# The decode's K pages multiplied with their queries on GpSimd instead of VectorE

## The chip, the cores and the metric

The kernel runs on one core of one Trainium2 chip. The metric is the device time of one launch in microseconds (us), lower is better. The core's engines are named as the profile names them: PE is TensorE, ACT ScalarE, DVE VectorE, POOL GpSimd, and SP is the engine that only issues DMAs here.

## The reference

One inference step of a two-layer decoder, for 512 prompt positions and for 8 sequences that each decode one token. Layer 0 is a convolution module with memory attention and a dense SwiGLU; layer 1 is stick-breaking attention over shared K/V with memory attention, then top-2-of-8 experts. The change lies in layer 1's stick-breaking attention:

```python
z = jnp.einsum('bthd,bshd->bhts', q, k) * HEAD_DIM ** -0.5 + bias
log_keep = jnp.where(causal, jax.nn.log_sigmoid(-z), 0.0)
between = lax.cumsum(log_keep, axis=3, reverse=True) - log_keep
w = jnp.where(causal, jnp.exp(jax.nn.log_sigmoid(z) + between), 0.0)
o = jnp.einsum('bhts,bshd->bthd', w, v)
# prompt: q, k of 512 new positions, 12 heads of 64.
# decode: 8 sequences; k and v are cache_k[page_table], cache_v[page_table]: 2 pages of 128 positions each
```

For a decoding sequence z is one query row against 256 cached keys: per page and head, 64 products and their sum.

## The kernel before

It is a hand-scheduled program: each engine has one list of instructions written out in order, and semaphores alone tie the lists together. The stages follow one another over the whole core: the projections up to layer 1's queries (to about 844 us of the span), stick-breaking attention (844 to 944), memory attention of layer 1 (to about 1000), the output projection, routing and the experts.

**The prompt's attention** is cut into 36 units (`UNITS`), one head and one group of query/key blocks each; `QGROUPS` gives three groups of 4, 3 and 3 blocks of 128, so a unit has 512 or 384 columns. Units go in pairs (a visit `v` holds units 2v and 2v+1), and six units make a period. For each unit u the engines pass data around:

- PE `stick_scores` (L2730): z into a PSUM bank; then ACT `soft_exp` (L1260) writes exp(z) to `zc`, DVE `soft_clamp` (L2015) clamps it in place, ACT `soft_log` (L1266) takes ln(1 + .), DVE `soft_max` (L2023) reads PSUM and `zc` and writes `sp`, ACT `soft_high` (L1272) rounds it to `sph`, DVE `soft_low` (L2032) subtracts the two into `spl`.
- PE `stick_sums` (L2747, L2749) adds the running sums of `sph` and of `spl` to z, ACT `stick` (L1280) takes the weights `wt`, and PE `stick_values` (L2764) multiplies them with V.

PE's order in visit v is: scores of visit v+2, sums of units 2v and 2v+1, values of visit v-1. The scores of visit v+3 wait (`sb_w`) until ACT has made `wt` of unit 2v+1, since six PSUM banks go round (`ZBANKS`). ACT's order in step s is exp of unit s, ln of s-1, rounding of s-2, `wt` of s-3. DVE's is clamp of s, max of s-1, low part of s-2, then a piece of the decode's work. Every sixth step has one more small piece for PE's finished output on ACT and on DVE (L1717).

**The decode's scores** ride in DVE's list. `pgs` holds for each sequence n two pages of K, 128 x 768 values each, and a buffer `qb` of two holds the query, copied to all partitions. From step 7 (`PAGES_FROM`) on three steps belong to one sequence: first `page_product` (L2008) multiplies both pages in place, one instruction of 1536 columns, then `page_scores` (L1999) sums one page over each head's 64 columns, and in the third step the other. The SP list loads the K pages, the first two queries, and then for each n, once both sums of n are done (`qk`), the two V pages over the K pages of n and the query of n+2. After step 31 the 8 sequences' scores get their bias, exp, ln and sums in the last steps of the prompt's units. GpSimd's list holds between the two clearings of `wpad` (L857, L858) and a clearing after the last unit (L860) nothing.

Of the kernel before, what the change touches and what calls it, by code (L numbers as in the profile page):

```python
# [25 lines left out]
ACT = mybir.ActivationFunctionType  # L26
ALU = mybir.AluOpType
# [3 lines left out]
P = 128  # L31
# [3 lines left out]
B = 8  # L35
# [7 lines left out]
FS = NH * HD // P  # L43
# [5 lines left out]
NPG = 2  # L49
# [54 lines left out]
def build(nc, a, o):  # L104
# [3 lines left out]
    with ExitStack() as ctx:  # L108
        def at(name, shape, dt, offset):
            return nc.alloc_sbuf_tensor_at(name, shape, dt, offset=base0 + offset)  # L110

        def small(name, shape, dt=F32):
            return ctx.enter_context(nc.sbuf_tensor(name, shape, dt))

        def sem(name):
            return ctx.enter_context(nc.semaphore(name))
# [63 lines left out]
        pgs = at("pgs", [P, B, NPG, FS * P], F32, 49920)  # L180
        qrow = at("qrow", [P, D], F32, 29120)
        qb = [at("qb0", [P, FS * P], F32, A + 87680), at("qb1", [P, FS * P], F32, A + 52608)]
# [5 lines left out]
        class Mem:  # L188
# [57 lines left out]
        rstd = small("rstd", [P, T])  # L246
# [93 lines left out]

        u_zero, ud_new, cv, cd, cd_sum = map(sem, "u_zero ud_new cv cd cd_sum".split())
        cw_in, cw_row, u_sh, wb_dve, wb_pool, cg, ce, ce_dve, ln_acc = map(sem, "cw_in cw_row u_sh wb_dve wb_pool cg ce ce_dve ln_acc".split())
        ln_sum, ln_mean, ln_xc, ln_sq, ln_used, ln_root, ln_rstd, ln_y = map(
            sem, "ln_sum ln_mean ln_xc ln_sq ln_used ln_root ln_rstd ln_y".split())
        outs = sem("outs")

        mk_in, mc_in, mv_in = map(sem, "mk_in mc_in mv_in".split())
# [7 lines left out]
        pg_in = [sem(f"pg_in{n}") for n in range(B)]  # L355
        qb_in = [sem("qb_in0"), sem("qb_in1")]
        sel_ready, qd_out, qm_in, qk, wp_zero, sd_pv, mix_hi, mix_lo = map(
            sem, "sel_ready qd_out qm_in qk wp_zero sd_pv mix_hi mix_lo".split())
# [93 lines left out]
        def row_broadcast(src, shape_ap):  # L452
            return bass.AP(tensor=src.tensor, offset=src.offset, ap=[[0, P]] + shape_ap)
# [36 lines left out]
        PG_AT = [0, 1, 4, 7, 2, 3, 5, 6]  # L490
# [16 lines left out]
        def _(e):  # L507
# [111 lines left out]
            def load_pages(src, n):  # L619
                for g in range(NPG):  # L620
                    page = e.value_load(ptab[0:1, bass.ds(n * NPG + g, 1)], min_val=0, max_val=src.shape[0] - 1)
                    e.dma_start(pgs[:, PG_AT[n], g:g + 1, :], src[bass.ds(page, 1)].rearrange("n s c -> s n c"))\
                        .then_inc(pg_in[n], 16)

            def load_query(n):
                e.dma_start(qb[n % 2][:, :], row_broadcast(qdr[n, 0:FS * P], [[1, FS * P]])).then_inc(qb_in[n % 2], 16)
# [15 lines left out]
            e.wait_ge(v_out, 32)  # L642
            load_query(1)
            for n in range(B):
                e.wait_ge(qk, 3 * n + 3)
                load_pages(vp, n)
                if n + 2 < B:
                    load_query(n + 2)

            e.wait_ge(sb_z, UNITS)  # L650
            e.wait_ge(sb_c, UNITS)
# [92 lines left out]
        def _(e):  # L744
# [111 lines left out]
            e.wait_ge(qd_out, 32)  # L856
            e.memset(wpad[0][:, :], 0.0).then_inc(wp_zero, 1)  # L857
            e.memset(wpad[1][:, :], 0.0).then_inc(wp_zero, 1)  # L858
            e.wait_ge(sb_c, UNITS)
            e.memset(memB.pdp[:, :, :], 0.0).then_inc(wp_zero, 1)  # L860
            for g in range(U_OUTB - 1, U_END - 1):
# [23 lines left out]
            for i in range(NT + 1):  # L885
                n = P if i < NT else B
# [64 lines left out]
        def _(e):  # L951
# [67 lines left out]
            n = 0  # L1019
# [131 lines left out]
            e.activation(halves(rstd[:, :]), ps[:, 0:2, 0:HALF], ACT.Ln, scale=1.0 / (FS * P), bias=eps[:, :])\  # L1151
             .then_inc(ln_root, 1)
            e.wait_ge(ln_root, 1)
            e.activation(rstd[:, :], rstd[:, :], ACT.Exp, scale=-0.5).then_inc(ln_rstd, 1)
            e.wait_ge(mb_step, MB_S)
            for c in range(FM):
                ins = e.activation(planes(hh[:, FS + c, :])[:, :, TP // PH:TQ],
# [213 lines left out]
            for i in range(NT + 1):  # L1371
                n = P if i < NT else B
# [113 lines left out]
            for k in range(4):  # L1486
                c, n = k // 2, k % 2
                e.activation(eyh[:, c, 512 * n:512 * n + 512], ps[:, 2 + k, :], ACT.Copy, scale=gsl[:, c:c + 1]).then_inc(f_act, 1)
            early_hi(4)
            for i in range(NF):  # L1490
                n = P if i < NT else B
# [10 lines left out]
        def _(e):  # L1502
# [211 lines left out]
            def mix_low(k, src, hi):  # L1714

                e.wait_ge(mix_hi, hi)
                e.tensor_tensor(hl[:, k, 0:TP], src, hh[:, k, 0:TP].bitcast(F32), ALU.subtract).then_inc(mix_lo, 1)  # L1717
# [68 lines left out]
            def decode_low_planes(q, hi):  # L1786

                e.wait_ge(mix_hi, hi)
                for c in range(FM):
                    ins = e.tensor_tensor(planes(hl[:, FS + c, :])[:, :, TP // PH:TQ],  # L1790
                                          ps[:, q, 64 + c * B:64 + c * B + B].rearrange("p (t g) -> p g t", g=PH),
                                          planes(hh[:, FS + c, :].bitcast(F32))[:, :, TP // PH:TQ], ALU.subtract)
                ins.then_inc(mix_lo, 1)
# [90 lines left out]
            mix_low_planes(FS + 1, ps[:, 7, :], 2)  # L1884
            e.wait_ge(ln_root, 1)
            decode_low_planes(3, 3)
            e.wait_ge(ln_rstd, 1)
            for k in range(FS):
                e.tensor_tensor(conv_out(k), conv_out(k), planes(rstd[:, :]), ALU.mult).then_inc(ln_y, 1)

# [103 lines left out]
            def pages(ap):  # L1994
                return ap.rearrange("p (g r) -> p g r", g=NPG)

            def page_scores(n, g):

                e.tensor_reduce(zd[:, 0, 96 * g + NH * n:96 * g + NH * n + NH],  # L1999
                                pgs[:, PG_AT[n], g, :].rearrange("p (h d) -> p h d", d=HD), AX, ALU.add)\  # L2000
                 .then_inc(qk, 1)

            def page_product(n):

                e.wait_ge(pg_in[n], 32)
                e.wait_ge(qb_in[n % 2], 16 * (n // 2 + 1))
                page = pgs[:, PG_AT[n], :, :]
                e.tensor_tensor(page, page, qb[n % 2][:, :].unsqueeze(1).to_broadcast([P, NPG, FS * P]), ALU.mult)\  # L2008
                 .then_inc(qk, 1)

            def soft_clamp(u):

                z = zc[:, u % ZBANKS, 0:unit_cols(u)]
                e.wait_ge(sb_e, u + 1)
                e.tensor_scalar(z, z, EXP_MAX, None, ALU.min).then_inc(sb_zc, 1)  # L2015

            def soft_max(u):

                h, n = unit(u)[0], unit_cols(u)
                e.wait_ge(sb_l, u + 1)  # L2020
                if u >= SP_SLOTS:
                    e.wait_ge(sb_lo, u - SP_SLOTS + 1)
                e.scalar_tensor_tensor(out=sp[:, u % SP_SLOTS, 0:n], in0=unit_z(u), scalar=bias[:, 0, h:h + 1],  # L2023
                                       in1=zc[:, u % ZBANKS, 0:n], op0=ALU.add, op1=ALU.max).then_inc(sb_s, 1)

            def soft_low(u):

                n = unit_cols(u)
                e.wait_ge(sb_hi, u + 1)
                if u >= SPL_SLOTS:  # L2030
                    e.wait_ge(sb_c, u - SPL_SLOTS + 1)
                e.tensor_tensor(spl[:, u % SPL_SLOTS, 0:n], sp[:, u % SP_SLOTS, 0:n], sph[:, u % ZBANKS, 0:n].bitcast(F32),  # L2032
                                ALU.subtract).then_inc(sb_lo, 1)

            PAGES_FROM = 2 * NQ + 1
            for s in range(UNITS + 2):
                if s < UNITS:
                    soft_clamp(s)
                if 1 <= s <= UNITS:
                    soft_max(s - 1)  # L2040
                if s >= 2:
                    soft_low(s - 2)
                n, part = (s - PAGES_FROM) // 3, (s - PAGES_FROM) % 3
                if 0 <= n < B:
                    if part == 0:
                        page_product(n)
                    else:
                        e.wait_ge(qk, 3 * n + 1)
                        page_scores(n, part - 1)
                if s == PAGES_FROM + 3 * B:  # L2050
                    e.wait_ge(qk, 3 * B)
                    e.tensor_tensor(pages(zd[:, 0, :]), pages(zd[:, 0, :]), bias2, ALU.add).then_inc(sd_step, 1)
                if s == UNITS - 3:
                    e.wait_ge(sd_step, SD_E)
                    e.tensor_scalar(zd[:, 1, :], zd[:, 1, :], EXP_MAX, None, ALU.min).then_inc(sd_step, 1)
                if s == UNITS - 1:
                    e.wait_ge(sd_step, SD_L)
                    e.tensor_tensor(zd[:, 1, :], zd[:, 0, :], zd[:, 1, :], ALU.max).then_inc(sd_step, 1)
                if s % (2 * NQ) == 4 and s >= 10:
                    f = (s - 10) // (2 * NQ)  # L2060
                    mix_low(f, ps[:, 6 + f % 2, :], MIX_ALL + f + 1)
# [125 lines left out]
            for i in range(NT + 1):  # L2187
                n = P if i < NT else B
# [161 lines left out]
            for k in range(4):  # L2350
                c, n = k // 2, k % 2
# [7 lines left out]
            for i in range(NF):  # L2359
                n = P if i < NT else B  # L2360
# [708 lines left out]
```

## Time and profile before

| | |
|---|---|
| median of 3 runs | 1744.93 us (1742.52 to 1746.0) |
| the profiled execution, its own time | 1747.19 us |
| its span in the trace | 1745.4 us |
| busy over the span: PE, DVE, ACT, POOL | 93%, 55%, 43%, 31% |
| mean granted clock of TensorE | 0.962 |

The shares are averages over stages with different limits; PE is near full in the projections and experts, which are most of the span. For a change in one stage the rows of that stage count. Times in the rows are us from the span's start, a row of the timeline gives start, duration, engine, line, operation, output and inputs, shape, and in brackets how long the engine was idle before it and what ended that. A duration in the timeline overlaps the next one's start a little, so what an instruction takes of its engine's time is read from start to start.

### The profile page before, as it was taken

How to read it: one execution, taken by the hardware profiler on the slowest of the kernel's cores; microseconds unless marked ns; L12 is line 12 of the kernel's file. 1: busy time of each engine (PE TensorE's matmuls, PEld its weight loads, DVE VectorE, ACT ScalarE, POOL GpSimd, SP SyncE). 2: the span in 40 equal slices, each digit the busy share in tenths (PEclk: the TensorE clock that was granted, in tenths of full speed). 3: DMA queues.
4: the chain of work that ended last, by engine and by line, in shares of the span. 5: the costliest groups of instructions: out<-in, count | busy, mean ns of one | idle time of the engine just before them, and what ended most of it. 6: DMA issues, size and time to landing. Idle time of an engine off the chain costs nothing.

```text
span 1745.4 us, 29562 instructions
## 1 busy us (share of the span) xinstructions
PE 1617.6 (93%) x11452; PEld 1493.9 (86%) x11452; DVE 955.1 (55%) x1248; ACT 757.0 (43%) x1067; POOL 539.2 (31%) x333
## 2 busy tenths in 40 slices
PE   6898878999999999899888797999999999999998
PEld 5898758999999999898765495989898898989896
DVE  6796554311111001522595627868677686868686
ACT  6445453322222122431585325455454455545454
POOL 1001213345554444232000131624152423415172
PEclk9899889999999999999999798999999999999989
DMA  6634202254454552121555216987979697997961
GB/s 205 114 96 149 77 1 73 73 150 138 138 150 135 165 166 94 50 96 58 207 161 143 99 40 179 308 229 241 257 224 270 208 294 201 265 233 232 256 237 51
DMA packets 346271, 282.01 MB, mean 162 GB/s; under 512 B 9505, under 2 KB 311117, under 8 KB 346055
## 3 DMA queue, kind: packets, MB, share of 16 engines
q1 hardware_dynamic: 324947, 251.09, 49.5%
q10 hardware_dynamic: 18084, 18.14, 3.1%
q0 software_dynamic: 3168, 11.80, 2.2%
q8 instruction: 46, 0.75, 0.2%
q14 instruction: 26, 0.21, 0.0%
HBM read 246.62 MB, written 35.10 MB: 161 GB/s over the span
## 4 chain that ended last, share of the span: by engine, by line
PE 78%; DVE 11%; issue 4%; ACT 3%; POOL 2%; SPq 1%; DMA 1%; ACTq 0%; DVEq 0%; POOLq 0%
PE ps L2412 35%; PE ps L2974 15%; PE ps L2977 7%; PE ps L2398 3%; PE ps L2400 3%; PE ps L2399 3%; PE ps L3001 2%; PE ps L3000 2%; DVE cT L1671 2%; PE ps L2551 2%; DVE wlo L1547 1%; PE ps L2380 1%; PE ps L2561 1%; DVE spl L2032 1%; DVE sp L2023 1%
## 5 line engine op out<-in xcount | busy, mean ns | idle before, releaser
L2974 PE MATMUL ps<-ejx,ewh 128*128 128x384 f32 x1408 | 404.5, 361 | 3.6 <-DVE ejx L2223 1.9
L2209 DVE TENSOR_TENSOR ewl<-eraw,ewh 128x2048 fp32r<-128x2048 f32 (+1 forms) x144 | 304.1, 2112 | 155.7 <-ACT ewh L1389 155.5
L1389 ACT ACTIVATE ewh<-eraw 128x2048 fp32r<-128x2048 f32 (+1 forms) x144 | 255.2, 1773 | 259.2 <-PE ps L2977 151.9
L2977 PE MATMUL ps<-ejx,ewl 128*128 128x192 f32 x1408 | 353.8, 251 | 0.0
L2412 PE MATMUL ps<-hh,whi 128*128 128x260 f32 x1504 | 312.4, 289 | 21.1 <-DVE hl L1912 16.5
L2412 PE MATMUL ps<-hh,wlo 128*128 128x260 f32 x1504 | 307.8, 287 | 0.0
L2412 PE MATMUL ps<-hl,whi 128*128 128x260 f32 x1504 | 307.8, 287 | 0.0
L896 POOL TENSOR_TENSOR ea<-eat,ea 128x128 fp32r<-128x128 f32 x88 | 171.7, 1951 | 341.6 <-ACT ea L1447 341.3
L2974 PEld LDWEIGHTS ps<-ejx,ewh 128*128 128x128 f32 x1408 | 266.0, 189 | 7.0 <-issue 7.0
L2977 PEld LDWEIGHTS ps<-ejx,ewl 128*128 128x128 f32 x1408 | 270.6, 192 | 0.0
L2412 PEld LDWEIGHTS ps<-hh,whi 128*128 128x128 f32 x1504 | 238.1, 193 | 24.7 <-issue 15.9
L2412 PEld LDWEIGHTS ps<-hh,wlo 128*128 128x128 f32 x1504 | 237.1, 193 | 0.0
L2412 PEld LDWEIGHTS ps<-hl,whi 128*128 128x128 f32 x1504 | 237.0, 193 | 0.0
L785 POOL TENSOR_TENSOR wlo<-raw,whi 128x2048 fp32r<-128x2048 f32 x36 | 165.9, 4610 | 110.4 <-ACT whi L1226 72.5
L1945 DVE TENSOR_TENSOR tmp<-ps,rstd 128x520 f32<-128x520 f32 x44 | 30.7, 699 | 198.8 <-PE ps L2412 194.9
L779 POOL TENSOR_TENSOR wlo<-raw,whi 128x2048 fp32r<-128x2048 f32 x13 | 59.6, 4586 | 171.0 <-ACT whi L958 171.0
L2412 PE MATMUL ps<-acth,whi 128*128 128x260 f32 x352 | 72.0, 286 | 4.1 <-POOL actl L826 4.1
L826 POOL TENSOR_TENSOR actl<-tmp,acth 128x520 f32 (+1 forms) x22 | 29.2, 1328 | 137.7 <-ACT acth L1197 137.7
L2412 PE MATMUL ps<-actl,whi 128*128 128x260 f32 x352 | 71.6, 285 | 0.0
L2412 PE MATMUL ps<-acth,wlo 128*128 128x260 f32 x352 | 71.5, 285 | 0.0
L2398 PE MATMUL ps<-ewh,ea 128*128 128x512 f32 x176 | 70.5, 401 | 0.0
L3001 PE MATMUL ps<-ewl,ea 128*64 128x512 f32 x176 | 70.2, 399 | 0.0
(440 smaller groups left out, 2531.6 us busy)
## 6 DMA issues: line engine op xcount, KB each, us to landing
eraw<-in_w_gate_e SPq DMA_DIRECT2D x88, 512.0 KB, 4.8
eraw<-in_w_up_e SPq DMA_DIRECT2D x88, 512.0 KB, 6.0
eraw<-in_w_down_e SPq DMA_DIRECT2D x64, 512.0 KB, 6.0
eraw<-in_w_down_e SPq DMA_DIRECT2D x48, 256.0 KB, 2.9
xs<-zero ACTq DMA_DIRECT2D x10, 1152.0 KB, 4.8
raw<-in_w_gate_d SPq DMA_DIRECT2D x22, 512.0 KB, 4.1
raw<-in_w_up_d SPq DMA_DIRECT2D x22, 512.0 KB, 5.3
raw<-in_w_down_d SPq DMA_DIRECT2D x16, 512.0 KB, 4.6
```

Source lines behind the costliest of these rows:

```text
L779: e.tensor_tensor(out=wlo[:, s, :], in0=raw[:, s, :], in1=whi[:, s, :].bitcast(F32), op=ALU.subtract).then_inc(w_lo, 1)
L785: e.tensor_tensor(out=wlo[:, s, :], in0=raw[:, s, :], in1=whi[:, s, :].bitcast(F32), op=ALU.subtract).then_inc(w_lo, 1)
L896: e.tensor_tensor(out=ea[:, m, C + CB:2 * C], in0=eat[:, m % 2, 0:P], in1=ea[:, m, 0:P].bitcast(F32), op=ALU.subtract)
L1389: e.activation(ewh[:, s, 0:n], eraw[:, u % RAW, 0:n], ACT.Copy).then_inc(ew_hi, 1)
L2209: e.tensor_tensor(ewl[:, s, 0:n], eraw[:, u % RAW, 0:n], ewh[:, s, 0:n].bitcast(F32), ALU.subtract)\
L2398: e.matmul(dst, w_hi_, x_hi, start=first, stop=False, skip_group_check=check)
L2399: e.matmul(dst, w_hi_, x_lo, start=False, stop=False, skip_group_check=check)
L2400: return e.matmul(dst, w_lo_, x_hi, start=False, stop=last, skip_group_check=check)
L2412: ins = e.matmul(ps[:, 2 * q + h, 0:HALF], w, xx[:, k, h * HALF:(h + 1) * HALF], start=opens, stop=closes)
L2974: e.matmul(ps[:, q, 0:2 * C], ewh[:, s, o:o + P], ejx[:, k, :, :].rearrange("p h n -> p (h n)"), start=(k == 0), stop=(k == KD - 1), skip_ ...
L2977: ins = e.matmul(ps[:, q, C:2 * C], ewl[:, s, o:o + P], ejx[:, k, 0, :], start=False, stop=(k == KD - 1), skip_group_check=True)
L3001: ins = e.matmul(ps[0:CB, 2 + c, :], ea[:, k, P:C], wlm, start=False, stop=(k == KE - 1), skip_group_check=True)
```

## The change

GpSimd gets the products: right behind the two clearings of `wpad` it waits for the pages and the query of sequence n and multiplies page by page, two instructions of 768 columns each, each announced on a new semaphore `qp`. DVE keeps the sums, in the same two of the three steps; the third step of each sequence is left with no decode work. `qk` counts sums alone. On SP the query of n+2 is now loaded once both products of n are done, and stands ahead of the wait for the sums of n and the loads of its V pages. A semaphore of layer 0 (`ln_rstd`) is folded into another (`ln_root`), which pays for the new one.

```diff
@@ sync
             for n in range(B):
-                e.wait_ge(qk, 3 * n + 3)
+                if n + 2 < B:
+                    e.wait_ge(qp, 2 * n + 2)
+                    load_query(n + 2)
+                e.wait_ge(qk, 2 * n + 2)
                 load_pages(vp, n)
-                if n + 2 < B:
-                    load_query(n + 2)
@@ gpsimd
             e.memset(wpad[1][:, :], 0.0).then_inc(wp_zero, 1)
+            for n in range(B):
+                e.wait_ge(pg_in[n], 32)
+                e.wait_ge(qb_in[n % 2], 16 * (n // 2 + 1))
+                for g in range(NPG):
+                    page = pgs[:, PG_AT[n], g, :]
+                    e.tensor_tensor(page, page, qb[n % 2][:, :], ALU.mult).then_inc(qp, 1)
             e.wait_ge(sb_c, UNITS)
@@ scalar, layer 0
-            e.activation(rstd[:, :], rstd[:, :], ACT.Exp, scale=-0.5).then_inc(ln_rstd, 1)
+            e.activation(rstd[:, :], rstd[:, :], ACT.Exp, scale=-0.5).then_inc(ln_root, 1)
@@ vector, layer 0
-            e.wait_ge(ln_rstd, 1)
+            e.wait_ge(ln_root, 2)
@@ vector
-            def page_product(n):
-
-                e.wait_ge(pg_in[n], 32)
-                e.wait_ge(qb_in[n % 2], 16 * (n // 2 + 1))
-                page = pgs[:, PG_AT[n], :, :]
-                e.tensor_tensor(page, page, qb[n % 2][:, :].unsqueeze(1).to_broadcast([P, NPG, FS * P]), ALU.mult)\
-                 .then_inc(qk, 1)
...
-                if 0 <= n < B:
-                    if part == 0:
-                        page_product(n)
-                    else:
-                        e.wait_ge(qk, 3 * n + 1)
-                        page_scores(n, part - 1)
+                if 0 <= n < B and part:
+                    e.wait_ge(qp, 2 * n + part)
+                    page_scores(n, part - 1)
                 if s == PAGES_FROM + 3 * B:
-                    e.wait_ge(qk, 3 * B)
+                    e.wait_ge(qk, 2 * B)
```

On DVE, at the first sequence, the list of before reads as follows (`zc` is the clamp, `sp` the max, `spl` the low part; L2008 is the product of both pages, L1999 the sum of one):

```order
L2032 TENSOR_TENSOR spl<-sp,sph 128x384 [waits sb_c,sb_hi]
L2008 TENSOR_TENSOR pgs<-pgs,qb_101 128x1536 [waits qb_in0,pg_in0]
L2015 TENSOR_SCALAR zc<-zc 128x384 [waits sb_e]
L2023 SCALAR_TENSOR_TENSOR sp<-ps,bias,zc 128x512 [waits sb_lo,sb_l]
L2032 TENSOR_TENSOR spl<-sp,sph 128x512 [waits sb_c,sb_hi]
L1999 TENSOR_REDUCE zd<-pgs 128x12 [waits qk]
L2015 TENSOR_SCALAR zc<-zc 128x384 [waits sb_e]
```

And the list of the change at the same place (all lines are shifted, L2007 is the sum):

```order
L2032 TENSOR_TENSOR spl<-sp,sph 128x384 [waits sb_c,sb_hi]
L2015 TENSOR_SCALAR zc<-zc 128x384 [waits sb_e]
L2023 SCALAR_TENSOR_TENSOR sp<-ps,bias,zc 128x512 [waits sb_lo,sb_l]
L2032 TENSOR_TENSOR spl<-sp,sph 128x512 [waits sb_c,sb_hi]
L2007 TENSOR_REDUCE zd<-pgs 128x12 [waits qp]
L2015 TENSOR_SCALAR zc<-zc 128x384 [waits sb_e]
```

The product with its two waits is gone, and the sum waits for GpSimd. On POOL, between the clearing of `wpad` and the clearing for the memory attention, the change has this where before there was nothing:

```order
L860 MEMSET wpad_105 128x280
L866 TENSOR_TENSOR pgs<-pgs,qb_101 128x768 [waits qb_in0,pg_in0]
L866 TENSOR_TENSOR pgs<-pgs,qb_101 128x768
L866 TENSOR_TENSOR pgs<-pgs,qb_102 128x768 [waits qb_in1,pg_in1]
L866 TENSOR_TENSOR pgs<-pgs,qb_102 128x768
```

Sixteen such instructions stand one behind the other, two for each sequence. On SP, behind the first two queries, the change has this; before, the third query stood behind both V loads:

```order
L627 DMA qb_102<-qdr 128x768 [waits v_out]
L627 DMA qb_101<-qdr 128x768 [waits qp]
L622 TENSOR_LOAD ptab [waits qk]
```

The third query moved ahead of the wait for the first sequence's sums and its V pages.

## Rows read from the trace of the kernel before

**Rows 1.** Windows: stretch, length, busy PE, PEld, DVE, ACT, POOL; granted clock; DMA

```profile
863.90:926.60 62.70, 50.39 (x483) 42.74 (x484) 62.70 (x102) 51.05 (x98) 0.00 (x0) 1.00 0.41 127
933.00:936.00 3.00, 1.34 (x9) 1.02 (x7) 2.25 (x5) 3.00 (x8) 0.00 (x0) 1.00 0.00 0
936.00:940.00 4.00, 3.91 (x24) 3.32 (x25) 2.48 (x6) 2.24 (x5) 0.00 (x0) 0.58 0.02 4
```

**Rows 2.** Timeline of DVE: the first product, and a piece of the steady state

```profile
863.87 1.76 DVE L2008 TENSOR_TENSOR pgs<-pgs,qb 128x1536 f32<-128x1536 f32 x1 [2.32 <-DMA qb<-qdr]
...
900.54 0.96 DVE L1999 TENSOR_REDUCE zd<-pgs 128x12 f32<-128x768 f32 x1
901.40 0.36 DVE L2015 TENSOR_SCALAR zc<-zc 128x384 f32<-128x384 f32 x1
901.67 0.62 DVE L2023 SCALAR_TENSOR_TENSOR sp<-ps,bias,zc 128x384 f32<-128x384 f32 x1
902.20 0.56 DVE L2032 TENSOR_TENSOR spl<-sp,sph 128x384 fp32r<-128x384 f32 x1
902.66 1.77 DVE L2008 TENSOR_TENSOR pgs<-pgs,qb 128x1536 f32<-128x1536 f32 x1
904.33 0.70 DVE L1717 TENSOR_TENSOR hl<-ps,hh 128x512 fp32r<-128x512 f32 x1
```

**Rows 3.** Waits from 863 to 927 us: total, times, longest

```profile
PE ps L2747 <- DVE spl L2032: 10.8, 13, 1.3
ACT wt L1280 <- PE ps L2749: 9.5, 14, 1.3
```

**Rows 4.** Timeline of PE: the start of the scores of visits 3, 4, 5, 6, 14, 15, 16

```profile
854.18 1.16 PE L2730 MATMUL ps<-qT,kT 64*128 64x128 f32 x16 [1.40 <-ACT wt L1280]
859.16 0.94 PE L2730 MATMUL ps<-qT,kT 64*128 64x128 f32 x12 [0.79 <-ACT wt L1280]
863.78 0.94 PE L2730 MATMUL ps<-qT,kT 64*128 64x128 f32 x12 [0.86 <-ACT wt L1280]
871.11 1.16 PE L2730 MATMUL ps<-qT,kT 64*128 64x128 f32 x16
...
912.54 0.94 PE L2730 MATMUL ps<-qT,kT 64*128 64x128 f32 x12 [0.38 <-ACT wt L1280]
918.09 1.16 PE L2730 MATMUL ps<-qT,kT 64*128 64x128 f32 x16
923.53 0.94 PE L2730 MATMUL ps<-qT,kT 64*128 64x128 f32 x12
```

**Rows 5.** POOL's groups: count, busy, mean ns, idle before

```profile
L779 POOL TENSOR_TENSOR wlo<-raw,whi 128x2048 fp32r<-128x2048 f32 x13 | 59.6, 4586 | 171.0 <-ACT whi L958 171.0
L814 POOL TENSOR_TENSOR wring<-wcol,id 128x1152 f32<-128x1152 f32 x6 | 13.4, 2247 | 100.0 <-PE ps L2551 100.0
L947 POOL TENSOR_TENSOR fw<-fw,xtk 128x1024 f32<-128x1024 f32 x2 | 4.8, 2390 | 22.4 <-DVE fw L2365 22.4
```

**Rows 6.** Timeline of DVE and of POOL in layer 0's memory attention

```profile
169.84 1.21 DVE L1728 TENSOR_TENSOR mkc<-mkc,mqb 128x1024 f32<-128x1024 f32 x1
171.09 1.22 DVE L1731 TENSOR_REDUCE mz<-mkc 128x16 f32<-128x1024 f32 x1
172.22 1.90 DVE L1728 TENSOR_TENSOR mkc<-mkc,mqb 128x1024 f32<-128x1024 f32 x1
...
170.24 2.80 POOL L814 TENSOR_TENSOR wring<-wcol,id 128x1152 f32<-128x1152 f32 x1 [1.74 <-PE ps L2551]
```

**Rows 7.** A tensor_scalar of DVE: min/median/max ns, then one, beside POOL's

```profile
L1747 DVE TENSOR_SCALAR mp<-mp,sts x32: 341/348/4715, 165.6 to 992.2; 128x256 f32<-128x256 f32 x32
...
987.06 4.71 DVE L1747 TENSOR_SCALAR mp<-mp,sts 128x256 f32<-128x256 f32 x1
987.10 4.53 POOL L779 TENSOR_TENSOR wlo<-raw,whi 128x2048 fp32r<-128x2048 f32 x1 [45.39 <-ACT whi L958]
```

**Rows 8.** The queries' DMAs: issue to landing, min/median/max

```profile
DMA to landing us min/median/max: 4.3/5.0/5.9
```

More of the change, by code:

```diff
@@ L342, in build @@
         cw_in, cw_row, u_sh, wb_dve, wb_pool, cg, ce, ce_dve, ln_acc = map(sem, "cw_in cw_row u_sh wb_dve wb_pool cg ce ce_dve ln_acc".split())
-        ln_sum, ln_mean, ln_xc, ln_sq, ln_used, ln_root, ln_rstd, ln_y = map(
-            sem, "ln_sum ln_mean ln_xc ln_sq ln_used ln_root ln_rstd ln_y".split())
+        ln_sum, ln_mean, ln_xc, ln_sq, ln_used, ln_root, ln_y = map(
+            sem, "ln_sum ln_mean ln_xc ln_sq ln_used ln_root ln_y".split())
+        qp = sem("qp")
         outs = sem("outs")
```

## The prediction

> **What bounds the kernel now.** I read the windows first, then DVE's timeline, then the waits, and last PE's scores. The stretch from 863.9 to 926.6, where the decode's pages are worked on, is DVE's: it is busy 62.70 of 62.70 us, PE 50.39, ACT 51.05, POOL not at all [rows 1]. The waits say the same: PE's sums stood 10.8 us for DVE's low part; ACT's 9.5 us for PE's sums come behind that [rows 3]. In the timeline DVE's instructions follow each other with no bracket between them [rows 2]. So DVE's time is the stage's time here, and the stages before and after can only shift.
>
> The question is how much of DVE's time could be given back before something else bounds. PE's score starts show it [rows 4]. There is a second loop without decode work in it: PE's sums of the even unit, then five ACT instructions in a row (wt, exp, ln, rounding, wt), then PE's next scores. Before the pages begin, at visits 3 to 5, DVE has idle time, and the brackets name ACT: 854.18 to 859.16 is 4.98, 859.16 to 863.78 is 4.62. In the page stretch the visit that corresponds to the first takes 923.53 - 918.09 = 5.44, the third kind 918.09 - 912.54 = 5.55, its price with DVE out of the way unknown, at most that. The second kind is bound by the loop in both places. So a period costs 15.62 now (5.44 + 4.62 + 5.55, rounded) and at best about 15.15 with DVE free. Only 0.46 a period is to be had, plus the irregular first visit, 871.11 - 863.78 = 7.33 instead of 5.55.
>
> **What is removed.** Eight products. One takes from 902.66 to 904.33, 1.67 us of DVE [rows 2]: 13.4 us. Also the wait of 2.32 us for the first query, in which DVE stood [rows 2].
>
> **What is added on GpSimd: its price.** The trace has no multiply of 768 columns on POOL. The nearest row is L947, two plain f32 tiles of 1024 columns in place, 2.39 us; L779 gives 4.59 for 2048 [rows 5]. The two lie on a line of 0.19 + 0.00215 a column, which makes 1.84 for 768; I take 1.85. The cheapest bound is L814, whose inputs are broadcast: 2.25 for 1152, which is 1.5 for 768 if all of it scales. The dearest is L947 scaled alone, 1.79, or with the 0.67 of waiting that POOL had in [rows 6] (2.80, where the other five of the group have (13.4 - 2.80) / 5 = 2.13), 2.5. Sixteen at 1.85 are 29.6 us of 62.7: GpSimd has the time.
>
> **What is added on DVE: standing still.** This term decides. In [rows 6] a DVE multiply of two SBUF tiles takes 1.21. The same instruction at 172.22 takes 1.90, and ends at 174.12: that is 1.08 behind POOL's end at 173.04. It did not run slower, it stood until POOL's was done. The reduce at 171.09, beside the same POOL instruction, took its 1.22. In [rows 7] a tensor_scalar, 0.348 in the median, takes 4.71 while POOL's runs from 987.10 to 991.63. And POOL's 2.80 at 170.24 begins while DVE's multiply runs to 171.05: it waited too. So one of the two engines holds something for a whole instruction, and DVE's clamp (tensor_scalar in SBUF) and low part (two SBUF inputs) are of the kinds that stood; max and L1717 have one input in PSUM, and the sum is a reduce, which I take as free.
>
> Where does a POOL product begin? When DVE lets go, at the end of a clamp or a low part that a free instruction follows. Pitches are from [rows 2]: clamp 0.27, max 0.53, low 0.46, sum 0.86. After a clamp, max runs for 0.53, and the low part then stands 1.85 - 0.53 = 1.32. After a low part that a sum follows, the clamp stands 1.85 - 0.86 = 0.99. Products come in pairs, so I take one of each: 1.16 a product. Between two POOL instructions I let the waiting DVE instruction go first; no row shows DVE waiting there for long.
>
> The Trainium skill ("GPSIMD Engine Reference", section 2.1 Instruction dispatch) gives about 2.5 cycles an element as the floor of a two-input instruction; with the 1.2 GHz of its page "SBUF — State Buffer" (the table of doors) that would be an estimate of 1.6 us for 768 columns. The trace has 2.39 for 1024 where that rule has 2.1. By the skill's figure each product would hold DVE 0.25 less, 4 us over all sixteen, and the sum below would be +5 rather than +9.
>
> **The ledger, from DVE's last low part before the first product (863.87 - 2.32 = 861.6, [rows 2]) to the end of the stretch at 926.6.**
> - Products gone: -13.4.
> - The start: -2.3 of wait. The query lands at 863.9 as before, DVE meanwhile does step 8, about 1.5 of work in 2.4 us, so 0.9 is waiting for ACT, and then its first sum stands for the first product, 864.0 to 865.9: +0.9 + 1.9. Together +0.5.
> - Fifteen further products: 15 x 1.16 = +17.4.
> - Windows without a product. GpSimd runs ahead. The query of n+2 is issued only behind the wait for the sums of n-1 and its V loads, and lands 5.0 later [rows 8]; so four pages' products go in the first 20 us, then come three with the pace of the sums, and products are done about two sequences before the sums are. That leaves about three windows of three steps with no product in them. There DVE needs (15.62 - 2 x 1.67) / 2 = 6.14, the loop of ACT and PE half of 15.15, 7.58: DVE idles 1.4 each, +4.2.
>
> Sum: -13.4 + 0.5 + 17.4 + 4.2 = +8.7. I also followed the four lists by hand with these pitches: when the first eight products are through, DVE is about 5.8 late; the rest adds 2 to 3. The two ways agree.
>
> Behind the stage nothing has slack that would take this up: the memory attention's DMAs are issued behind the last unit, and the V pages are used there or later. The folded semaphore changes nothing: both waits were for the same ACT instructions. SP's query moved up costs nothing, as it waits for landing 5 us ahead of use.
>
> The ledger is against the profiled execution's 1747.19 (span 1745.4), which lies 2.3 over the median; I put the difference on the median: 1744.93 + 8.7, about **1754**.
>
> **TensorE's clock.** At 933 to 936 PE was busy 1.34 of 3.00, and then the granted clock fell to half: 0.58 as a mean over 936 to 940 [rows 1]. The change makes such holes: between the first products the low parts of two units are late by over a microsecond each, so PE stands for 2 to 3 us at a time. At half the clock PE's 80% of need becomes 160%, so a stretch of 3.4 us at half (0.84 of 4 us, from the mean 0.58) gives away about 1.3. None to four such falls: 0 to +5. In the centre I leave it out, in the range it is in.
>
> **Rivals.**
> - *The two engines run side by side, as the change means.* Then DVE has 49 us of work and the loop of ACT and PE bounds: -1.8 at the first visit (7.33 to 5.55), -0.46 for each of four visits of the first kind, so -3.6; about 1741. For it: the clamp itself was never seen beside POOL. Against it: rows 6 and 7 show both kinds of instruction standing. Chance 0.09. It is decided by the blocked time per product: under (13.4 - 4.2 - 0.5) / 15 = 0.58 us it is faster.
> - *Half of it is hidden.* If products cost 1.5 (the bound from L814), the blocked time is 0.81 and the ledger gives -13.4 + 0.2 + 12.2 + 4.2 = +3.2; if, besides, only the low part is held and the clamp is not, every second hold disappears, and it ends within 0.2%, at 1743 to 1748. Chance 0.14.
> - *DVE is starved:* POOL's next product takes its turn before the waiting DVE instruction, so a page costs DVE 3.7 minus 0.5 in one piece. That is 8 x 3.2 = 25.4 instead of 17.4, +8 more, 1762. For it: POOL's two products have no wait between them. Against it: nothing either way. Chance 0.12.
> - *The forecast*, holds as in the ledger with 0 to 3 for the clock: 1749 to 1759, chance 0.65.
>
> **The numbers.** Likeliest 1754. The range reaches from the hidden case (1744) to the starved one with the clock (1765); 0.09 lies below it, a few hundredths above. A measurement here tells about 0.2% (3.5 us) from no change. Faster by more than that: the side-by-side rival at its best, 0.09. Within: 0.14. Slower: 0.77.
>
> **What the profile after would show.** POOL's L866 at 1.85 each where DVE is quiet, longer where it waited. The clamp and the low part with mean durations about half a microsecond over their 0.36 and 0.56 and maxima near 1.9, while max, sum and L1717 keep theirs. The stretch to the bias about 9 us longer, and all later stages as long as now. PE's wait for the low part well over 10.8. Were the clamp and low part as long as before, the side-by-side rival holds. If the time is up but the holes sit at the sum, waiting for `qp`, then it is GpSimd's pace, not the holding, that is at fault.

## The result, and the profile after

The change makes the kernel slower: 1753.99 us in the median of 5 runs (1753.53 to 1756.35) against 1745.46 for the kernel before (1742.52 to 1746.63), a ratio of 1.0051 with a 95% interval of 1.0039 to 1.0063. The forecast was 1754 (1744 to 1765). The profiled execution spans 1752.1 us, 6.7 more than before. One launch of all those behind this document, in the second run of halves with the later start, took 5346 us; its median counts that launch, its ratio leaves it out, and nothing here explains it.

The windows of the changed kernel, over the stretch that now holds the sixteen products and the sums (columns as in [rows 1]), and then three pairs of neighbouring stretches:

```profile
863.90:933.70 69.80, 53.72 (x469) 45.67 (x469) 62.97 (x90) 49.25 (x95) 29.91 (x16) 0.93 0.37 114
...
867.00:870.40 3.40, 1.50 (x16) 1.30 (x16) 3.40 (x4) 1.31 (x3) 3.40 (x2) 1.00 0.45 120
870.40:873.80 3.40, 3.40 (x26) 3.04 (x22) 3.40 (x5) 2.07 (x5) 3.40 (x3) 0.52 0.67 180
...
898.00:901.10 3.10, 1.48 (x18) 1.18 (x20) 3.10 (x7) 2.36 (x6) 0.16 (x1) 1.00 0.53 138
901.10:904.50 3.40, 3.40 (x21) 3.08 (x20) 3.11 (x5) 1.13 (x3) 0.00 (x0) 0.52 0.64 226
...
914.70:918.10 3.40, 1.10 (x6) 0.76 (x6) 3.40 (x6) 2.34 (x4) 1.51 (x1) 1.00 0.27 72
918.10:921.50 3.40, 3.40 (x29) 2.83 (x27) 3.40 (x7) 2.07 (x4) 0.00 (x0) 0.53 0.47 159
```

DVE is busy for 62.97 us, as much as the 62.70 before, though eight products are gone from it. And three times the granted clock of TensorE falls from its upper level (2.4 GHz) to half of it (1.2), behind stretches in which PE had been busy for 1.50 of 3.40, 1.48 of 3.10 and 1.10 of 3.40 us. In [rows 1] it was whole over the corresponding 62.7 us.

DVE's groups from 855 to 945 show where its time went (mean ns of one is the second number behind the bar):

```profile
L2032 DVE TENSOR_TENSOR spl<-sp,sph 128x384 fp32r<-128x384 f32 x22 | 18.9, 858 | 0.0
L2007 DVE TENSOR_REDUCE zd<-pgs 128x12 f32<-128x768 f32 x16 | 15.1, 941 | 1.7 <-POOL pgs L866 1.7
L2023 DVE SCALAR_TENSOR_TENSOR sp<-ps,bias,zc 128x384 f32<-128x384 f32 x21 | 12.8, 611 | 0.8
L2015 DVE TENSOR_SCALAR zc<-zc 128x384 f32<-128x384 f32 x20 | 11.0, 548 | 7.8 <-ACT zc L1268 7.8
L2032 DVE TENSOR_TENSOR spl<-sp,sph 128x512 fp32r<-128x512 f32 x10 | 7.9, 786 | 0.0
L2015 DVE TENSOR_SCALAR zc<-zc 128x512 f32<-128x512 f32 x10 | 6.5, 646 | 2.1 <-ACT zc L1268 2.1
L1725 DVE TENSOR_TENSOR hl<-ps,hh 128x512 fp32r<-128x512 f32 x5 | 3.4, 684 | 1.1 <-ACT hh L1102 1.1
```

The sum, the max and L1725 (before: L1717) take what they took in [rows 2]. The low part of 384 columns has gone from 0.56 to 0.858 in the mean, the clamp from 0.36 to 0.548. One piece of DVE's timeline shows single ones:

```profile
868.77 0.94 DVE L2007 TENSOR_REDUCE zd<-pgs 128x12 f32<-128x768 f32 x1
869.63 1.12 DVE L2015 TENSOR_SCALAR zc<-zc 128x384 f32<-128x384 f32 x1
870.67 0.60 DVE L2023 SCALAR_TENSOR_TENSOR sp<-ps,bias,zc 128x384 f32<-128x384 f32 x1
871.20 1.65 DVE L2032 TENSOR_TENSOR spl<-sp,sph 128x384 fp32r<-128x384 f32 x1
872.77 0.68 DVE L1725 TENSOR_TENSOR hl<-ps,hh 128x512 fp32r<-128x512 f32 x1
```

Behind the sum the clamp is longer by 1.12 - 0.36 = 0.76, behind the max the low part by 1.65 - 0.55 = 1.10: the two kinds of standing that the prediction named. GpSimd's products on that kernel, minimum, median and maximum:

```profile
L866 POOL TENSOR_TENSOR pgs<-pgs,qb x16: 1815/1938/2281, 862.6 to 914.1; 128x768 f32<-128x768 f32 x16
```

The waits from 863 to 936, to be read beside [rows 3] (total, times, longest):

```profile
ACT wt L1288 <- PE ps L2746: 19.3, 16, 3.0
...
PE ps L2744 <- DVE spl L2032: 12.7, 10, 2.9
...
DVE zd L2007 <- POOL pgs L866: 1.7, 1, 1.7
```

PE's wait for the low part has grown little in total (10.8 to 12.7), but its longest from 1.3 to 2.9, and the three stretches ahead of the falls are such holes. DVE waited for GpSimd's pace once, 1.7 us, at the first sum.

### The profile page after: what moved, and what is told of

Same layout as the page of the kernel before. It is cut to its first block, busy times and chain, and to the rows that moved or that the text cites. A ratio compares the mean times of both kernels' runs of the same rounds, so it can differ in the third digit from the quotient of the medians.

```text
span 1752.1 us, 29570 instructions
## 1 busy us (share of the span) xinstructions
PE 1620.4 (92%) x11452; PEld 1496.3 (85%) x11452; DVE 957.7 (55%) x1240; ACT 756.8 (43%) x1067; POOL 570.5 (33%) x349
## 4 chain that ended last, share of the span: by engine, by line
PE 79%; DVE 10%; issue 3%; ACT 3%; POOL 2%; SPq 1%; DMA 1%; ACTq 0%; DVEq 0%; POOLq 0%
PE ps L2409 35%; PE ps L2971 15%; PE ps L2974 7%; PE ps L2395 3%; PE ps L2396 3%; PE ps L2397 3%; PE ps L2998 2%; PE ps L2997 2%; DVE cT L1679 2%; PE ps L2548 2%; DVE wlo L1555 1%; PE ps L2377 1%; DVE spl L2032 1%; PE ps L2558 1%; PE ps L2577 1%
```

## The experiments

All times are medians; each ratio is against runs of the kernel before on the same chip.

**No products.** Nothing is multiplied on either engine, so the decode's scores are wrong; the rest of the change stays.

```diff
                 for g in range(NPG):
-                    page = pgs[:, PG_AT[n], g, :]
-                    e.tensor_tensor(page, page, qb[n % 2][:, :], ALU.mult).then_inc(qp, 1)
+                    e.sem_inc(qp, 1)
```

> The change with the products left out altogether: GpSimd waits for pages and query and announces them, but multiplies nothing, so the decode's K scores are sums of the pages themselves. VectorE keeps its sums. Holding theory: without POOL instructions no clamp and no low part stands (maxima as before, 0.45 and 0.69), and the loop of ACT and PE is the bound, which the prediction put at 15.15 a period and about 1741 us in all, 12 to 13 under the change. Rival, that the moved waits or the load order of the queries cost the time: it stays within 2 us of the change's 1754.

Measured: 1740.36, ratio 0.9976 (0.9965 to 0.9988). The clamps and low parts of 384 columns take 356 and 548 ns in the mean. PE's scores start like this, from the timeline:

```profile
885.30 1.16 PE L2726 MATMUL ps<-qT,kT 64*128 64x128 f32 x16 [0.67 <-ACT wt L1287]
890.28 0.94 PE L2726 MATMUL ps<-qT,kT 64*128 64x128 f32 x12 [0.75 <-ACT wt L1287]
894.89 0.94 PE L2726 MATMUL ps<-qT,kT 64*128 64x128 f32 x12 [0.75 <-ACT wt L1287]
900.43 1.16 PE L2726 MATMUL ps<-qT,kT 64*128 64x128 f32 x16 [0.66 <-ACT wt L1287]
```

The reader is to see the period of the free loop, 900.43 - 885.30 = 15.13, and that every start waits for ACT's `wt`, none for DVE. The third kind of visit, whose free price the prediction did not know, takes 5.54. So the moved waits, the semaphores and the loads cost nothing that can be told; what costs is that GpSimd multiplies. This is also about the least that any placing of the products can take with these lists, but for the clock: in this profile too it falls once, behind the decode's bias (0.86 in the mean from 933 to 945).

**Spare multiplies beside the kernel before.** VectorE keeps all products, GpSimd multiplies 16 times on tiles that nothing reads.

```diff
             e.memset(wpad[1][:, :], 0.0).then_inc(wp_zero, 1)
+            spare = tmp[:, :, :].rearrange("p a t -> p (a t)")
+            for n in range(B):
+                e.wait_ge(pg_in[n], 32)
+                e.wait_ge(qb_in[n % 2], 16 * (n // 2 + 1))
+                for g in range(NPG):
+                    e.tensor_tensor(spare[:, 0:768], spare[:, 0:768], spare[:, 768:1536], ALU.mult).then_inc(qp, 1)
+                    e.wait_ge(qp, 2 * n + g + 1)
```

(Left out: the new semaphore `qp` and the folding of `ln_rstd` into `ln_root` that pays for it, as in the change.)

> The kernel before, VectorE still does all products, and GpSimd does sixteen multiplies of 768 columns beside it on spare tiles that nothing reads, each after the one before, released by the same pages and queries. Holding theory: VectorE is full here, so each of the sixteen multiplies costs what a clamp, a low part or a product stands, 0.8 to 1.1 us: plus 13 to 18, about 1760. Rival, that only the handing over (the waits for the products) cost time in the change: about 1745, no difference to the kernel before.

Measured: 1764.86, ratio 1.0120 (1.0103 to 1.0137), 19 us more. The groups of DVE from 855 to 945:

```profile
L2040 DVE TENSOR_TENSOR spl<-sp,sph 128x384 fp32r<-128x384 f32 x18 | 15.4, 854 | 0.0
...
L2016 DVE TENSOR_TENSOR pgs<-pgs,qb 128x1536 f32<-128x1536 f32 x8 | 14.0, 1747 | 2.4 <-DMA qb<-qdr 2.4
L2023 DVE TENSOR_SCALAR zc<-zc 128x384 f32<-128x384 f32 x17 | 11.0, 649 | 2.4 <-ACT zc L1268 2.4
```

Nothing is handed over between the engines here, and the same two kinds of instruction are longer. Against before (both shapes of each) they stand 14.9 us in this window. I had expected VectorE's products to stand too, and none did. The timeline says why: the first began at 861.49, GpSimd's multiply at 861.54, and it was GpSimd's that took 3.38 where the shortest takes 1.81; when the other seven began, no GpSimd instruction was running. So this run does not test whether such a product can be held; in [rows 6] one of 1024 columns was. The remaining 4 to 5 us I put down to the clock, without a run of its own: its windows show 0.70 over 863 to 880 and 0.57 over 895 to 915.

**Clearing instead of multiplying.** As the last, but GpSimd only writes.

```diff
-                    e.tensor_tensor(spare[:, 0:768], spare[:, 0:768], spare[:, 768:1536], ALU.mult).then_inc(qp, 1)
+                    e.memset(spare[:, 0:2080], 0.0).then_inc(qp, 1)
```

> As the run with spare multiplies, but GpSimd clears 2080 columns each time (about 1.8 us by the 1.81 of the 2048-column clearing early in the kernel), so it writes SBUF and reads nothing. Holding of everything by any GpSimd instruction: clamps, low parts and products all stand again, plus 13 to 18. Rival by the Trainium skill (SBUF - State Buffer, Who interferes with whom): an instruction with two SBUF inputs is held only by a GpSimd instruction that reads, a tensor_scalar in its fast mode by any; then low parts and products keep their 0.69 and 1.77, only clamps stand, and where the clearing starts under a product or a sum less of it is left: plus 5 to 12.

Measured: 1753.47, ratio 1.0053 (1.0036 to 1.0069). DVE's groups from 855 to 945, then GpSimd's:

```profile
L2023 DVE TENSOR_SCALAR zc<-zc 128x384 f32<-128x384 f32 x20 | 11.9, 593 | 3.7 <-ACT zc L1268 3.7
L2040 DVE TENSOR_TENSOR spl<-sp,sph 128x384 fp32r<-128x384 f32 x21 | 11.4, 544 | 0.0
...
L865 POOL MEMSET tmp<- 128x2080 f32 x16 | 30.2, 1888 | 42.8 <-DMA qb<-qdr 42.3
```

The clamps stand (593 ns in the mean where 0.36 us is normal, single ones up to 2.06 us), the low parts do not (544 ns). So it is not one lock on everything: here the low part, with two SBUF inputs, stood for GpSimd's multiply and not for its clearing, and the clamp stood for both.

The Trainium skill ("SBUF — State Buffer", section "Who interferes with whom") says that an instruction with two SBUF inputs contends only with a GpSimd instruction that reads SBUF, and one in a two-port mode with any. The trace agrees: 544 ns for the low parts, 593 for the clamps; that the clamp runs in such a mode no run shows.

The clamps' standing is 20 x (0.593 - 0.356) + 10 x (0.580 - 0.423) = 6.3 us, against the durations of the run without products; the kernel is 8 to 9 slower. The 2 to 3 us between have no run of their own; the clock falls three times in this profile too (0.93 over 863 to 933).

**The queries loaded in the order of before.**

```diff
             for n in range(B):
-                if n + 2 < B:
-                    e.wait_ge(qp, 2 * n + 2)
-                    load_query(n + 2)
                 e.wait_ge(qk, 2 * n + 2)
                 load_pages(vp, n)
+                if n + 2 < B:
+                    load_query(n + 2)
```

> The change with the loads on SP in the order of before: the query of n+2 behind the V pages of n, and so behind the sums of n. Products are then done just one to two sequences ahead instead of two to three. Holding theory: the same sixteen holds, 1752 to 1756, unless a query comes too late; the sums of n+2 begin one sequence (8 us) after those of n end, the query needs about 7, the product 3.7, so the first sum of each may stand 1 to 3 us: up to 1765. Rival, that the moved loads cost time in the change: 1748 or less.

Measured: 1756.00, ratio 1.0072 (1.0053 to 1.0091), its interval overlaps the change's. So the moved load neither makes the cost nor takes it away.

**Halves and quarters.** The same columns on GpSimd in 32 or 64 instructions.

```diff
                 for g in range(NPG):
-                    page = pgs[:, PG_AT[n], g, :]
-                    e.tensor_tensor(page, page, qb[n % 2][:, :], ALU.mult).then_inc(qp, 1)
+                    for c in range(0, FS * P, 384):
+                        page = pgs[:, PG_AT[n], g, c:c + 384]
+                        e.tensor_tensor(page, page, qb[n % 2][:, c:c + 384], ALU.mult).then_inc(qp, 1)
```

(and the waits on `qp` count twice as far; quarters have 192 for 384 and four times.)

> The change, each page's product cut into two POOL instructions of 384 columns, 32 in all. Holding theory: the hold of a whole page, read as 0.53 + 1.13 = 1.66 and 0.86 + 0.76 = 1.62 us, becomes about 0.83; behind a clamp 0.83 - 0.53 = 0.30 is left to stand, behind a low part with a sum 0. Most of the 14 us of standing goes away, at most 16 x 0.30 + a few = 5 to 7 remain, and the loop of ACT and PE bounds: 1742 to 1746, about 10 under the change, at or under the kernel before. Rival, a cost that goes with columns on GpSimd or with GpSimd's pace: 32 instructions take longer in sum than 16, so 1754 or more.

> The change with each page's product cut into four POOL instructions of 192 columns, 64 in all. Holding theory: a hold of about 0.42 is shorter than the max that follows a clamp (0.53), nothing should stand for more than a tenth or two, unless an instruction meets POOL's without a free one ahead of it; 1741 to 1745, like the kernel without products. GpSimd needs 64 x about 0.6 = 38 us of some 60, enough. Rival as for halves: 1754 or more.

Measured: halves 1743.34, ratio 0.9997 (0.9984 to 1.0009); quarters 1745.20, ratio 1.0004 (0.9993 to 1.0015). The cost of the change is gone in both, with the same multiplications on the same engine. The halves' groups of DVE, then of GpSimd, from 855 to 945:

```profile
L2033 DVE TENSOR_TENSOR spl<-sp,sph 128x384 fp32r<-128x384 f32 x23 | 14.9, 647 | 0.4 <-ACT sph L1281 0.4
L2016 DVE TENSOR_SCALAR zc<-zc 128x384 f32<-128x384 f32 x21 | 10.5, 498 | 3.7 <-ACT zc L1269 3.7
...
L867 POOL TENSOR_TENSOR pgs<-pgs,qb 128x384 f32<-128x384 f32 x32 | 37.3, 1198 | 24.6 <-DMA qb<-qdr 24.6
```

Over the run without products the clamps and low parts (both shapes) stand 7.2 us in all with halves and 6.9 with quarters, where the change has 13.9. In the halves a low part of 384 columns behind a max takes 0.83 (871.44 in DVE's timeline) where 0.55 is normal, so it stands 0.28, as expected. For quarters I had expected next to nothing, and that was wrong: their shortest is 0.58, so the second of a row begins about where the max (0.53) ends, and the low part meets it. That is argued from the durations, not shown by a run.

**Halves, and the sums one step later.** With halves the first sum waited 2.7 us for its product, and the first visit took 7.33 as before the change.

```diff
-            PAGES_FROM = 2 * NQ + 1
+            PAGES_FROM = 2 * NQ + 2
```

> Halves as before, and the decode's sums begin one step later (PAGES_FROM 8 instead of 7). In the run with halves the first sum stood 2.7 us for GpSimd's first halves, and the visit from 864.2 took 7.33 as in the kernel before, where the free loop takes 5.54. One step later the first sum finds its product ready or nearly: 1 to 1.8 us less than halves, 1741 to 1742.5, near the kernel without products. Rival, that the first visit is long for the holds and not for the first sum's wait: no difference to halves.

> Halves with the sums one step later once more, in five rounds beside the two others: 1740 to 1742, as the kernel without products, 3 to 5 under the kernel before.

Measured: 1740.57, ratio 0.9980 (0.9968 to 0.9992), and again in five rounds 1742.57, ratio 0.9981 (0.9970 to 0.9991) beside a before of 1746.09. That is as fast as the kernel without any product. In neither profile does the clock fall between 863 and 933, nor behind it, where it fell in the run without products. Windows of TensorE alone (length, busy PE, granted clock, DMA share and GB/s), the run without products first and then the second run of this one:

```profile
863.00:933.00 70.00, 57.23 (x559) 1.00 0.42 132
933.00:945.00 12.00, 10.82 (x81) 0.86 0.33 99
...
863.00:933.00 70.00, 57.95 (x555) 1.00 0.42 130
933.00:945.00 12.00, 9.51 (x81) 1.00 0.41 102
```

That is part of why the two are level. Up to the decode's bias even plain halves are 2.0 us longer than no products (78.1 from DVE's first clamp against 76.1). Behind the bias, to DVE's last instruction on `zd`, they need 15.3 where the run without products needs 16.8 with its fall. So halves still cost something, and it is hidden by a fall that does not come.

How much of the later start's own gain is the clock's is open. Over the whole stage, from the first clamp to that last instruction, the two profiles with the later start take 92.7 and 93.1 us and the one with plain halves 93.4. But that one is among the quickest of its ten executions: four with a mean clock of 0.965 or 0.966 took 1741.1 to 1741.6 us, the six with 0.959 to 0.963 took 1742.8 to 1748.6.

**One step later, with whole pages, and with the products on VectorE.** The same one-line edit on the change and on the kernel before.

> The change with whole pages, and the decode's sums begin one step later (PAGES_FROM 8 instead of 7). Holding theory: the sixteen holds stay, 14 us of standing in clamps and low parts, the clock falls too; only the first sum's 1.7 us goes: 1751 to 1754. Rival, that the start was the main cost of the change as it was in the run with halves: 1746 or less.

> The kernel before, all products on VectorE, with the decode's work one step later. The wait of 2.32 us for the first query goes, the first visit should shrink from 7.33 to 5.6. If it is the start that made halves-and-later fast, this gives the same, 1741 to 1743. If VectorE's load counts (its period of 15.62 against the free 15.14, four times), it stays about 2 us behind: 1743 to 1744.

Measured: whole pages on GpSimd 1750.78, ratio 1.0033 (1.0020 to 1.0046); the kernel before with the edit 1745.06, ratio 0.9997 (0.9988 to 1.0006). So the later start alone gives nothing when VectorE multiplies, and with whole pages the change stays slower. Only both together, short GpSimd instructions and the later start, come out clear of the kernel before. Of the whole pages' 1751 to 1754 the low end came. For the kernel before I had expected 1743 to 1744; it gained nothing that can be told. Its first visit did shrink, from 7.33 to 5.62. But the clock falls twice between 863 and 933 in its profile, where the kernel before has no fall, and once behind, as there:

```profile
863.00:933.00 70.00, 59.30 (x533) 0.95 0.40 125
933.00:945.00 12.00, 9.63 (x74) 0.86 0.34 91
```

The stage takes 96.9 us, and 96.8 before. That the later start is worth nothing to VectorE's own products is therefore what was measured, but by this one profile the falls may have eaten what the first visit gave.

## Why the prediction was right

**What bounds the stage.** Right. The free loop was put at 15.15 a period from visits before the pages and is 15.13 in the run without products; the gain if both engines ran side by side was put at about 4 us and that run gave 0.24%, 4.2 us. The room above the kernel before was as small as the prediction said, which is why a modest cost was enough to turn the change.

**The standing.** The mechanism was right and its size too large. The ledger had 17.4 us, 1.16 for each of fifteen products. Against the run without products the four groups of the change are longer by 22 x (0.858 - 0.548) + 10 x (0.786 - 0.681) for the low parts and 20 x (0.548 - 0.356) + 10 x (0.646 - 0.423) for the clamps, 13.9 us. Seven clamps and seven low parts stood; one product ran while DVE was idle, and for the first the sum waited. A single standing is mostly 0.76 or 1.10, where the ledger had 0.99 and 1.32; a few begin otherwise, under another instruction or out of an idle stretch, and take 0.91 to 1.43. The reason for the size is in the numbers: 0.86 of sum + 0.76 is 1.62, 0.53 of max + 1.10 is 1.63. A product holds DVE for 1.62 us, though GpSimd's shortest takes 1.82. I had taken the whole for the hold.

The Trainium skill's floor ("GPSIMD Engine Reference", section 2.1 Instruction dispatch), of which the prediction made an estimate of 1.6 us and which its sum did not use, agrees with the trace for the hold, 1.62. The sum by it was +5; what it would have missed is the clock, below.

One sign was misjudged. The means were to rise by about half a microsecond; those of 384 columns rose by 0.19 and 0.30, since only 10 of the 42 in these groups stood. The longest, 1.67 and 1.97, are about the 1.9 that was named.

**The clock.** Left out of the centre, and it should have been in. It fell three times in the stretch. Behind the second and the third fall DVE waits for ACT for 2.24 us each; in the one window without a product where the clock was whole, that wait is 0.67:

```profile
887.55 1.67 DVE L2015 TENSOR_SCALAR zc<-zc 128x384 f32<-128x384 f32 x1 [0.67 <-ACT zc L1268]
...
906.45 0.40 DVE L2015 TENSOR_SCALAR zc<-zc 128x384 f32<-128x384 f32 x1 [2.24 <-ACT zc L1268]
...
924.51 0.36 DVE L2015 TENSOR_SCALAR zc<-zc 128x384 f32<-128x384 f32 x1 [2.24 <-ACT zc L1268]
```

Twice 1.57 is 3.1 us, in the range of 0 to 5 that the prediction gave it. That price is read from one execution; no run held the clock and kept the holds. All executions on record allow a second estimate. Over the 61 of the kernel before that were run beside the experiments, time falls as the mean clock rises, by 7.2 us for 0.01 (6.3 to 8.2 on the three chips). The change's five have 0.9596 in the mean, those 0.9629, which makes 2.4 us, as an estimate.

The clock's share is about what the standing was over-sized by, 3.5. So the sum hit as closely as it did because two terms were off in opposite directions; that is luck.

**The sum.** From the low part before the first product to the bias it was to be +8.7. Before, and then after (timeline of DVE):

```profile
861.00 0.55 DVE L2032 TENSOR_TENSOR spl<-sp,sph 128x384 fp32r<-128x384 f32 x1
...
926.30 0.38 DVE L2052 TENSOR_TENSOR zd<-zd,bias 128x192 f32<-128x192 f32 x1
```

```profile
859.80 0.55 DVE L2032 TENSOR_TENSOR spl<-sp,sph 128x384 fp32r<-128x384 f32 x1
...
933.40 0.36 DVE L2049 TENSOR_TENSOR zd<-zd,bias 128x192 f32<-128x192 f32 x1
```

65.3 has become 73.6, +8.3. By the timelines it is made of -13.4 for the products, +14.1 for the fourteen standings one by one, +6.0 of idle time with a bracket (8.3 against 2.3), and 1.6 in shorter gaps. Of the 8.3 the span shows 6.7: the stages before happened to be 1.2 quicker in the execution profiled, and from the bias to the end of the stage it was 1.2 quicker, since in the kernel before the clock fell just behind the bias [rows 1] and here it did not; the stages behind were 0.8 longer. The medians differ by 8.5.

**Windows without a product.** They were there: GpSimd is idle for 6.4 us ahead of the fifth sequence and is through with its last product at 916.2, while the last sum starts at 931.1. But their size was right only with the clock in it. At the start DVE idled 2.6 us where the ledger had 2.8. In the windows it idled 5.7 where the ledger had 4.2, and 3.1 of the 5.7 are those already counted under the clock; 2.6 are left, so this term too was over-sized, by 1.6. The 1.6 of short gaps, which the ledger did not have, make up for that.

**The rivals.** Side by side is refuted by the fourteen standings and by the spare multiplies. "Half of it is hidden" had two halves: that the clamp is not held is refuted, seven stood; that a product blocks less than GpSimd's whole 1.85 was so (1.62). Starvation did not come: in the piece above, the clamp at 869.63 and the low part at 871.20 each stood for one product and then went (in that rival's sum 3.7 is the price of a sequence's two pages, not of one). That GpSimd's pace was at fault, named as the sign to look for, is 1.7 us at the first sum and nothing elsewhere; with the later start it is gone. By the ratios (1.0051 and 1.0033) that run is about 3 us ahead of the change, but their intervals overlap.

## What to carry to other kernels

Moving work from VectorE to GpSimd paid here only by what GpSimd did while VectorE was idle or in instructions that kept their time beside it: the max and L1725 with an input in PSUM, and the sum, a reduce (0.611, 0.684 and 0.941 us with the products, 0.62, 0.70 and 0.96 before). Count, for each GpSimd instruction, how long such a stretch is and how much of the hold is left over. If the hold is longer than those stretches, cut the GpSimd instruction until it fits about one of them: here cutting each in two turned +0.5% into level, and into a gain of 0.2% together with giving the first product time to arrive. When two such kernels are compared, look at TensorE's clock in each profile first: one fall was worth 1.2 to 1.6 us here, as much as some of the differences read. And price the removal by the next loop, not by the busy time removed: 13.4 us left VectorE, and only 4 were to be had.

## What was not expected of the hardware

- A multiply of 768 columns on GpSimd held VectorE for 1.62 us (0.53 + 1.10 and 0.86 + 0.76), less than its own 1.82 at the shortest.
- GpSimd can be the one that stands: its first spare multiply, begun 0.05 us behind VectorE's product (two SBUF inputs, 1536 columns), took 3.38 us, and that product its usual 1.76.
- Cutting finer did not help further: 64 pieces stood 6.9 us, 32 pieces 7.2, 16 pieces 13.9.
- Halves with the later start still stood 10.2 and 11.5 us in the two profiles by their groups (637 and 842 ns for the low parts, 614 and 662 for the clamps, in the second), against the change's 13.9, and the kernel was as fast as without products. In part VectorE stood in time in which it would have idled: its idle time ahead of the clamps is 5.3 us from 855 to 945, and 9.4 without products. In part it is the clock, as told at that run.
- Whole pages with the later start stood 15.5 us, and the clock fell twice. Their stage takes 99.9 us, 6.7 more than the second run of halves with that start; 4.0 of it is the standing, and two falls at 1.57 would be 3.1.
